# Modulation slots moved into the expert stages, a barrier taken out before the second projection, and a reordered first chunk in the third mixer

## The reference, cut to what matters

```python
# first stack, layer l: six modulation vectors of each stream from one product
sh1, sc1, g1, sh2, sc2, g2 = split(silu(c) @ w_mod[l] + b_mod[l], 6)
h  = x * (1 + sc1) + sh1
x  = layer_norm(ALPHA * x + g1 * mixer(h), ln_g[l, 0], ln_b[l, 0])
h2 = x * (1 + sc2) + sh2
x  = layer_norm(ALPHA * x + g2 * moe(h2, ...), ln_g[l, 1], ln_b[l, 1])
# second layer's mixer (l = 1): q, k, v = split(h @ w_in_odd), then attention
# second stack, third mixer: a gated delta rule over chunks of 16, 128 and 128 tokens;
# in each chunk a triangular system is inverted and the state of the heads is carried on
```

## Time and profile before

| | |
|---|---|
| three timed runs | 2897.89, 2899.05, 2900.29 us; median 2899.05 us |
| the profiled execution | 2899.31 us, its span 2897.4 us |
| busy in it | PE 92%, DVE 68%, ACT 52%, POOL 4% |
| chain that ended last, by engine | PE 77%, DVE 6%, ACT 5%, issue 3%, DMA 1% |
| mean granted clock of PE | 0.956 of full speed |

### The profile page before, as it was taken

One profiled execution on the slowest core, in us unless ns is written; L12 is line 12 of the kernel. 1 busy time (PEld: TensorE's weight loads), 2 busy tenths in 40 slices (PEclk: granted clock), 3 DMA queues, 4 the chain that ended last, 5 costly groups with the idle time before them and its releaser, 6 DMA issues.

```text
span 2897.4 us, 55092 instructions
## 1 busy us (share of the span) xinstructions
PE 2667.6 (92%) x21144; PEld 2425.4 (84%) x21144; DVE 1967.3 (68%) x3487; ACT 1501.9 (52%) x2540; POOL 124.1 (4%) x149
## 2 busy tenths in 40 slices
PE   6988889996897999889899998999988899998999
PEld 4845579995766999779699988999888799997999
DVE  2167479996365999764667774677866577766677
ACT  3256368884454888654543454434742343445433
POOL 1010011100000111000000020000000000000000
PEclk8999889997997999989899999999989999999999
DMA  8281279995633999654055542455540155542453
GB/s 298 88 305 59 78 253 378 364 364 219 204 131 128 354 358 361 252 160 147 30 164 175 170 127 92 163 175 170 165 131 1 59 167 175 165 132 74 160 188 117
DMA packets 286158, 528.98 MB, mean 183 GB/s; under 512 B 14288, under 2 KB 207104, under 8 KB 285328
## 3 DMA queue, kind: packets, MB, share of 16 engines
q1 hardware_dynamic: 273312, 499.77, 50.2%
q0 software_dynamic: 9216, 12.61, 1.3%
q10 hardware_dynamic: 3440, 13.98, 1.3%
HBM read 526.21 MB, written 21.06 MB: 189 GB/s over the span
## 4 chain that ended last, share of the span: by engine, by line
PE 77%; DVE 6%; ACT 5%; issue 3%; DMA 1%; ACTq 0%; PEld 0%; PEldq 0%; DVEq 0%; POOLq 0%
PE ps L2335 17%; PE ps L2903 6%; PE ps L2904 6%; PE ps L2905 6%; PE ps L1959 4%; PE ps L1961 4%; PE ps L1960 4%; PE ps L2923 3%; PE ps L2925 3%; PE ps L2924 3%; PE ps L1995 2%; PE ps L1996 2%; PE ps L1997 2%; PE ps L564 2%; PE ps L951 1%
## 5 line engine op out<-in xcount | busy, mean ns | idle before, releaser
L2335 PE MATMUL ps<-H_part,W_hi 128*128 128x272 f32 (+2 forms) x2160 | 490.4, 305 | 25.9 <-DVE H_part L2239 13.1
L2134 DVE TENSOR_TENSOR W_lo<-ring,W_hi 128x1024 fp32r<-128x1024 f32 x384 | 452.8, 1222 | 45.3 <-ACT W_hi L2056 44.3
L2952 ACT ACTIVATE W_hi<-ring 128x1024 fp32r<-128x1024 f32 x264 | 263.1, 1049 | 294.0 <-PE ps L2925 185.7
L2903 PE MATMUL ps<-room_part,W_hi 128*128 128x272 f32 (+1 forms) x1408 | 404.6, 287 | 5.0 <-DVE room_part L2239 5.0
L2056 ACT ACTIVATE W_hi<-ring 128x1024 fp32r<-128x1024 f32 x384 | 384.7, 1052 | 39.0 <-PE ps L1961 18.1
L2904 PE MATMUL ps<-room_part,W_hi 128*128 128x272 f32 (+1 forms) x1408 | 403.5, 287 | 0.0
L2905 PE MATMUL ps<-room_part,W_lo 128*128 128x272 f32 (+1 forms) x1408 | 402.8, 286 | 0.0
L2335 PEld LDWEIGHTS ps<-H_part,W_hi 128*128 128x128 f32 x2160 | 361.2, 192 | 46.1 <-issue 30.4
L2335 PE MATMUL ps<-H_part,W_lo 128*128 128x272 f32 (+2 forms) x1216 | 359.8, 296 | 0.0
L2992 DVE TENSOR_TENSOR W_lo<-ring,W_hi 128x1024 fp32r<-128x1024 f32 x264 | 314.1, 1219 | 10.4 <-ACT W_hi L2952 9.4
L2308 DVE TENSOR_TENSOR W_lo<-ring,W_hi 128x1024 fp32r<-128x1024 f32 x186 | 224.4, 1247 | 120.5 <-ACT W_hi L2300 120.1
(11 more groups left out here) (520 smaller groups left out, 5480.6 us busy)
## 6 DMA issues: line engine op xcount, KB each, us to landing
ring<-in_w_down SPq DMA_DIRECT2D x108, 1024.0 KB, 5.4
ring<-in_w_gate_up SPq DMA_DIRECT2D x88, 1024.0 KB, 5.1
ring<-in_w_gate SPq DMA_DIRECT2D x64, 1024.0 KB, 7.3
ring<-in_w_up SPq DMA_DIRECT2D x64, 1024.0 KB, 7.4
ring<-in_w_mod SPq DMA_DIRECT2D x48, 1024.0 KB, 5.7
ring<-in_fox_w_in SPq DMA_DIRECT2D x32, 1024.0 KB, 5.6
ring<-in_gdn_w_in SPq DMA_DIRECT2D x16, 1024.0 KB, 5.7
ring<-in_gla_w_in SPq DMA_DIRECT2D x12, 1024.0 KB, 5.4
```

The source lines that it names most:

```text
L2134: dve.tensor_tensor(lo, c.ring[:, (self.g0 + p) % SLOTS, W], hi.bitcast(F32), ALU.subtract)\
L2335: mm = pe.matmul(self.out(i), a, b, start=(k == 0 and n_part == 0), stop=(k == KC - 1 and n_part == 2))
L2903: pe.matmul(out, wh[:, k, M], hi, start=(k == 0), stop=False)
L2952: act.activation(self.slot_parts(p)[0][:, C], c.ring[:, g % SLOTS, C], ACT.Copy).then_inc(c.hi_done, 1)
```

## The change

The 48 slots are spread differently. The first expert stage does slots 32 to 35 at its end, the norm behind it 36 to 39, `OddHeads` 40 to 43 and the second expert stage 44 to 47. Within an expert stage PE's products stand behind the last `down`, ACT's copy between the last expert's rows and the loads of `outputs`, and DVE's `begin` and `finish` ahead of the additions; SP issues the four loads behind the stage's last weights. SP also issues two of the norm's four loads ahead of its wait for `outputs`.

`Project` gets `flows = True`, so that there is no barrier between norm and projection. The norm runs `project.upper(act, 0)` behind the square root and `project.lower(dve, 0)` behind the normalising multiplications. In place of the barrier, the split of chunk `k` waits until `X` of chunk `k` is written (`ACC` and `ACC_part` are the same memory), and `X` of chunks 5 to 7 is written between the splits. The norm's `begin` moves to the start of DVE's part, `finish` into `Project.vector`, and ACT's copy behind `H` of chunk 5.

In the first chunk of the third mixer `EB` moves behind ACT's last level copy, `KD` behind the copies of level 2 (the banks of keys and values are exchanged so that they stay untouched), and the 16 multiplications by `EB` move from DVE to POOL. The second chunk waits for POOL (`faded`).

```diff
 class Project(Stage):
+        self.norm, norm.project, self.flows = norm, self, True
...
     def scalar(self, act):
-        upper(0)
+        rest = norm.X_SCALAR[True]
         for k in range(KC):
+            if k in rest:
+                act.wait_ge(self.scalar_done, self.act.at("x", k))
+            else:
+                act.wait_ge(norm.vector_done, norm.dve.at("x", k))
             act.activation(self.parts[0][k][:, T], self.src[:, k, T], ACT.Copy)\
                .then_inc(self.scalar_done, self.act.mark("src", k))
+            if k + 3 in rest:
+                act.activation(norm.x_out(k + 3), self.c.ACC[:, k + 3, T], ACT.Identity, bias=norm.b[k + 3], scale=norm.g[k + 3])\
+                   .then_inc(self.scalar_done, self.act.mark("x", k + 3))
...
     def vector(self, dve):
-        dve.tensor_scalar(dst, gain, factor, None, ALU.mult).then_inc(self.vector_done, self.dve.mark("scaled"))
-        lower(0)
         for k in range(KC):
...
-        for s in range(1, len(self.sources)):
-            lower(s)
+        dve.tensor_scalar(dst, gain, factor, None, ALU.mult).then_inc(self.vector_done, self.dve.mark("scaled"))
+        self.lower(dve, 1)
+        norm.mods.finish(dve, norm.dve)
+        for s in range(2, len(self.sources)):
+            self.lower(dve, s)
...
 class LayerNorm(Stage):
     def sync(self, sp):
+        if self.mods:
+            self.mods.sync(sp, 0, 2)
         for t in range(self.experts.nt):
             sp.wait_ge(self.experts.outputs_in[t], 32)
         if self.mods:
-            self.mods.sync(sp)
+            self.mods.sync(sp, 2)
...
+        if self.project:
+            self.project.upper(act, 0)
...
+                if self.mods and k == 5:
+                    self.mods.scalar(act, 0, 1)
...
+        if self.project:
+            self.project.lower(dve, 0)
...
 class FeedForward(Stage):
         self.load(sp, "D", self.N - 1)
+        self.mods.sync(sp)
...
     def gathered_tensor(self, pe):
+        self.mods.tensor(pe, 0, 1)
         for t in range(self.nt):
             pe.wait_ge(self.picks_added, t + 1)
...
     def gathered_scalar(self, act):
         ye(EXPERTS - 1)
+        self.mods.scalar(act, 0, 1)
         self.rows_landed(act)
...
     def gathered_vector(self, dve):
+        self.mods.begin(dve)
+        added = StageCount(c.count(f"gathered_mods{self.layer}"), 0)
+        self.mods.finish(dve, added)
+        dve.wait_ge(added.count.sem, added.at("gate"))
...
 class GdnChunk(Stage):
+        self.keys, self.values = (6, 4) if t == 0 else (4, 6)
...
         if self.t > 0:
+            if self.t == 1:
+                pe.wait_ge(self.faded.sem, self.faded.at(7))
...
+            if self.t == 0:
+                pe.wait_ge(self.scalar_done, self.act.at("kd"))
...
-            if self.t == 0:
-                if l == 1:
-                    dve.wait_ge(self.scalar_done, self.act.at("eb"))
-                later = slice(n, T2)
-                for h in range(8 * (l - 1) // (self.levels - 1), 8 * l // (self.levels - 1)):
-                    dve.tensor_tensor(m["QE"][:, h, later], m["Q"][:, h, 3 + n:3 + T2], m["EB"][:, h, later], ALU.mult)
-                    dve.tensor_tensor(m["KBE"][:, h, later], m["KB"][:, h, later], m["EB"][:, h, later], ALU.mult)
...
+    def pool(self, pool):
+        if self.t == 0:
+            m, n = self.m, self.tn
+            later = slice(n, T2)
+            pool.wait_ge(self.scalar_done, self.act.at("eb"))
+            for h in range(8):
+                pool.tensor_tensor(m["KBE"][:, h, later], m["KB"][:, h, later], m["EB"][:, h, later], ALU.mult)
+                pool.tensor_tensor(m["QE"][:, h, later], m["Q"][:, h, 3 + n:3 + T2], m["EB"][:, h, later], ALU.mult)\
+                    .then_inc(self.faded.sem, self.faded.mark(h))
...
-        if self.t == 0:
-            act.activation(m["EB"], m["BB"], ACT.Exp).then_inc(self.scalar_done, self.act.mark("eb"))
...
+            if self.t == 0 and l == 3:
+                act.activation(m["EB"], m["BB"], ACT.Exp).then_inc(self.scalar_done, self.act.mark("eb"))
+            if self.t == 0 and l == 2:
+                kd().then_inc(self.scalar_done, self.act.mark("kd"))
...
-    yield LayerNorm(c, 0, [(0, 0), (1, CTX)], (1, 0), behind, mods=ModSlots(c, 32, 8, at=14856, banks=(0, 1, 2), turned=3))
+    norm = LayerNorm(c, 0, [(0, 0), (1, CTX)], (1, 0), behind, mods=ModSlots(c, 36, 4, at=14856, banks=(0,), turned=4))
...
+    stage.mods = ModSlots(c, first, 4, at=14856, banks=(0,), turned=3)
```

More of the change, by code:

```diff
@@ L394, in __init__, with sync @@
         self.pick = core.room[:, at - 2 * self.FOUR:at]
-    def sync(self, sp):
-        for s in range(self.n):
+    def sync(self, sp, first=0, last=None):
+        for s in range(self.n)[first:last]:
             layer, n = divmod(self.first + s, self.PER_LAYER)
@@ L4036, in first_stack @@
     w = d["w_in_odd"]
-    yield Project(c, c.H, [columns(w, s * WIDE) for s in range(6)],
+    yield Project(c, norm, c.H, [columns(w, s * WIDE) for s in range(6)],
                   [(h // 2, "feature", h % 2 * P, P, CTX, SEQ, squared(Q[:, h, CTX:T1], sq_q[:, h, :], m["qn"])) for h in range(8)]
@@ L4051, in first_stack, with experts @@
     yield norm
-    behind = yield from experts(c, norm, 1, CTX, SEQ)
+    behind = yield from experts(c, norm, 1, CTX, SEQ, 44)
     yield LayerNorm(c, 1, [(1, CTX)], None, behind, shift_to=META)
-def experts(c, behind, layer, t0, tn):
+def experts(c, behind, layer, t0, tn, first):
     d = c.dram
```

79 lines of the change are left out of this document (43 added, 36 removed).

## The result

| | before | changed |
|---|---|---|
| median (runs) | 2898.47 us (4) | 2876.87 us (4), 2874.21 to 2877.56 |
| profiled execution, its span | 2899.31, 2897.4 us | 2877.56, 2875.8 us |

The account below looks back on a forecast made before the run. PE, the busiest engine, was taken to bound the kernel, so its waits were the places to gain. 12.3 + 3.9 + 3.8 - 1.0 - 0.2 = 18.8 us less gave 2880.3 from the median, stated as 2880.5, range 2875.0 to 2887.5.

Parts of the forecast that it names:

- Norm and projection, 12.3: Norm and the projection behind it: the last low part of `H` ends at 733.9 instead of 746.2, 12.3 us gained.
- That ACT paces the first output: Projection: PE starts some 14 us earlier, but ACT's splits pace its first output, which takes 1.8 us back.
- OddHeads, 3.9 (2.5 to 4.6): `OddHeads`: four products and one turn go, 4.4 us; DVE's idle time limits the gain to 3.9, bounds 2.5 and 4.6.
- The chunk, 3.8: Third mixer's first chunk: 2.7 us at the first level plus 2.2 from DVE, less 1.1 for `KD` between copies.
- Ends of the expert stages, -1.0 and -0.2: Expert stages' ends: an early load beside the last scatter costs 1.0 us (0 to 5.5), modulation copies 0.2 (at most 1.5).
- the signs that I named: Expected in the changed profile, among others: last scatter landing within 5 us, last addition of `OddHeads` 15 to 16 us earlier.
- The rival that had this price (3 to 5 us more): Ends of the expert stages: scatter at its contended time and both copies late, 2883 to 2887 us; chance 0.13.
- The clock, 0 and up to 3 of loss: Projection's first two outputs: a clock rising late in the second loses 1 to 3 us; taken as 0.
- the clock helps: Rival: in the chunk or `OddHeads` the clock does not fall, up to 4 us gained, 2874 to 2877; chance 0.08.
- forecast case: Whole kernel: the terms hold about as costed, 2877 to 2884 us; chance 0.61.
- POOL as the bound (slower), 0.02: Second chunk: PE waits for POOL from 1.36 us per multiplication; at 3 us each the kernel takes 2907; chance 0.02.
- it does not do what it says, 0.05: Norm's path is held elsewhere, so only `OddHeads` and the chunk gain: 2892 to 2898 us; chance 0.05.

Follow-up runs that it names:

- slots_only: The kernel before with only the modulation slots moved; barrier, load order and split weights as before: 2887.3 us, ratio 0.9958.
- best1: late_loads with, in the chunk, `KD` behind the copies of level 3 and `EB` between the two output copies: 2873.5 us, ratio 0.9916.
- pool3: The changed kernel with each of POOL's 16 multiplications of the chunk done three times: 2891.4 us, ratio 0.9972.
- odd8: The changed kernel with eight modulation slots in `OddHeads` and none in the second expert stage: 2878.7 us, ratio 0.9927.
- late_loads: The changed kernel with both of the norm's early modulation loads behind the wait for `outputs`: 2872.0 us, ratio 0.9904.
- late_again: late_loads measured once more, beside the changed kernel on the same chip: 2871.5 us, ratio 0.9907.
- one_early: The changed kernel with one of the norm's modulation loads ahead of the wait for `outputs` instead of two: 2871.8 us, ratio 0.991.
- chunk_alone: The kernel before with only the edits of the third mixer's first chunk: 2891.6 us, ratio 0.9974.
- before_again: The kernel before, unchanged, run once more for one profile: 2904.6 us (one run).

## Why the prediction was right, point by point

**Norm and projection, 12.3.** Measured up to the last low part of `H` 12.1 us (from the norm's start: before 39.96, changed 27.85); 11.4 at `OddHeads`, and 11.2 to 12.6 in the profiles named above. The difference of 0.7 is the clock: low until about 736.3, 0.7 us into the second output, where before it had risen 0.9 us ahead of it; one of the cases of loss that I had named (1 to 3) and set at 0. In the profiles whose clock rose as early as before, the whole 12.1 stayed. That ACT paces the first output was half right: at the low clock PE's three products take 0.64 us, as long as ACT's split of 0.61, so PE waited only twice for 0.22. The term was right, and its make-up differs from what I had in mind: 60% of it, 7.4 us in slots_only, comes with the move of the slots alone, which I would have put at 3.9.

**OddHeads, 3.9 (2.5 to 4.6).** 3.25 in the profile, in the bounds, but for two errors that cancel. The work is worth 4.9, above my upper bound; the clock took 1.6. The bound failed where it let DVE give back only the idle of the earlier trace rows: DVE also lost 0.36 us of wait for the last turn, its eight sums take 4.35 us together instead of 4.86 (slots_only against before), and `finish` is 0.2 shorter on half the columns. The sums' lengths are not their own. Each starts while POOL multiplies and ends 0.28 us behind that multiplication (0.28 to 0.30 in all 24 of before, slots_only and the changed kernel), and without POOL a sum takes 0.36 to 0.41; two of them in before, DVE and then POOL:

```profile
807.25 0.62 DVE L722 TENSOR_TENSOR room<-room 128x256 f32<-128x256 f32 x1
807.80 0.41 DVE L733 TENSOR_TENSOR room<-ps,small 128x256 f32<-128x256 f32 x1
808.13 0.52 DVE L722 TENSOR_TENSOR room<-room 128x256 f32<-128x256 f32 x1
```
```profile
806.96 1.41 POOL L746 TENSOR_TENSOR room<-room,small 128x256 f32<-128x256 f32 x2 [0.97 <-PE ps L686]
```

So POOL and DVE already waited for each other in `OddHeads`, in the kernel before, and I had costed such a wait only in the chunk.

**The chunk, 3.8.** 4.1 at its end, 3.65 behind the next one, where the clock came back later. By terms: at the first level 2.65 (2.7 forecast), behind it 1.45 (2.2 - 1.1 = 1.1). `KD` between the copies cost 0.7 (PE waited 0.63 there, and best1's chunk ends 0.7 sooner), not 1.1. POOL's 16 took 10.6 us and no one waited. Here the edit worked by a margin that I had not seen: I wrote that POOL works while DVE computes the next chunk's differences. In fact DVE starts them at 2145.51 and POOL ends at 2145.57. best1 and pool3 show what an overlap costs: 0.61 to 0.68 us each instead of 0.21. I had bounded that at a whole POOL instruction for each of the eight, 5 us, of which some 2.5 come through; best1 lost 3.8 on DVE, of which 0.7 came through. The Trainium skill, SBUF — State Buffer, Who interferes with whom, has both halves, and I had used only the one on two inputs: by it a `tensor_scalar` in a two-port mode also takes the pair of ports that DVE shares with GpSimd, and whoever comes second waits for the whole instruction. Both traces agree, in both directions (DVE's 0.21 to 0.68, POOL's 0.63 to 1.71).

**Ends of the expert stages, -1.0 and -0.2.** This step failed in size: the one load beside the scatter costs 2 to 5 us, 3.9 in the mean against the kernels with the slots moved and without it (2.2 in the profile of the changed kernel), and my 1.0 rested on the load's "share is gone by about 683". The traffic does thin out there, from 365 GB/s and a DMA share of 0.96 in the window 680 to 682 to 98 GB/s in the next, and still the scatter, issued at 679.2, landed 2.5 us later than alone:

```profile
680.00:682.00 2.00, 1.41 (x20) 0.71 (x12) 0.05 (x1) 0.38 (x1) 0.16 (x1) 1.00 0.96 365
682.00:684.00 2.00, 0.00 (x0) 0.00 (x0) 0.37 (x3) 0.00 (x0) 0.00 (x0) 1.00 0.25 98
```

What failed is the price of the time side by side: by the three recorded landings the scatter lands 0.5 to 0.9 us behind the load, as if it had to wait for nearly all of it (that it does is not shown). I should have taken a value near the middle of my bounds; of the signs that I named, the last scatter within 5 us failed (5.6, and up to 7.0), and so did the last addition of `OddHeads`, 13.6 us earlier instead of 15 to 16. The rival that had this price (3 to 5 us more) was closer than the forecast. The copy of ACT at 680.87 was in time for the loads at 684.92; in the second stage the scatter landed in 2.6 as before, and the cost of about 0.4, by odd8, is near the 0.2 said.

**The clock, 0 and up to 3 of loss.** It did both. Near the edits it took 0.7, 1.6 and 0.4 us; far from them it gave 5.1. The rival "the clock helps" named the chunk and `OddHeads`, where it did not help; the median fell into its 2874 to 2877, just below the forecast case, by other places. That is luck and not the rival's mechanism.

**POOL as the bound (slower), 0.02**, and **it does not do what it says, 0.05**: both out. pool3 shows that three times the work loses 14.4 us, so the mechanism exists, with 11.5 us of cover before it starts.

So the sum was right by compensation: my terms came to 18.8, the trace gives 16.8 for them and takes 1.1 back in the attention and the second expert stage (0.7 of it around that stage's first products, not looked into), and the late windows brought the rest, 5.1, for which I had no term.

## What to carry to other kernels

Cost an edit over a path at an equal clock: the same four products were worth 4.9 us, and showed as 3.25 or 6.5. When work leaves a path, look for every wait that stood behind it, transfers too; here they were as much as the work. A load that is moved ahead of a wait should be asked what else is in flight then: this kernel's early second load bought nothing and cost 2 to 5 us, and the three runs that differ from the changed kernel only in it (late_loads, late_again, one_early) are the fastest measured, 2871.5 to 2872.0. Before a part is called worth what its profile shows, compare that with the times of the executions that were not profiled: chunk_alone's was of an execution 4.4 us longer than most.

## What was not expected of the hardware

- DVE's `tensor_scalar` on 128 elements took 0.21 us alone and 0.61 to 0.68 us beside POOL multiplications of 0.63 to 0.75; beside DVE's two-input instructions of 1.22 to 1.28 us POOL's took 1.62 to 1.71. A DVE sum of two SBUF inputs (128x256) took 0.36 to 0.41 us alone and up to 0.62 beside a multiplication of POOL, and ended 0.28 us behind POOL's instruction each time.
- One load of 1 MB, issued 1.9 us ahead of an indirect scatter, made it land in 5.6 us instead of 3.1, and in five other profiles in 6.5 to 7.0.
- The clock loss at one place came in steps of 1.7 (1.7, 3.4, 5.1), also between two executions of one kernel (before and before_again, 1.7 and 5.1 at the first late place). Two low stretches, 100 and 500 us behind the last edit, are gone in all eight profiles of kernels with the new chunk and the rest of the change (pool3 apart) and there in all five without one of them.
